# Hybrid decoder layer: one VectorE product moved two slots up, and a state load issued earlier by GpSimd

## The reference, cut to what matters

```python
u = concat([gq, gk, gv])                     # pre-conv rows; the sample group has a cached halo of 3 rows
conv = silu(causal_depthwise_conv(u, conv_w))
q_g, k_g, v_g = l2norm(cq) * GDN_SCALE, l2norm(ck), cv
# per chunk of 64 tokens: solve (I + A) X = rhs with A strictly lower triangular, then update the state
o_gdn, s_gdn_new = gdn_scan(q_g, k_g, v_g, log_a, beta, state_gdn)
o_gdn = rmsnorm(o_gdn, gdn_norm_g) * silu(gz)        # silu(z) for each of a pair's two heads
merged = sigmoid(gate_a) * (o_hg @ w_out_hg) + sigmoid(gate_b) * (o_gdn @ w_out_gdn)
```

## Time and profile before

| what | value |
|---|---|
| median of three runs | 3566.07 us |
| the profiled execution's own time | 3569.11 us |
| its span, first to last instruction | 3567.6 us |
| TensorE matmul busy | 3483.7 us (98%) |
| VectorE / ScalarE / GpSimd busy | 2237.2 (63%) / 1797.9 (50%) / 846.7 (24%) us |
| moved by DMA | 588.08 MB, mean 165 GB/s |
| granted TensorE clock, mean | 0.994 |

### The profile page before, as it was taken

The page is one execution under the profiler, slowest core; times in us unless marked ns, Lnnn a source line. Parts: engine busy times, 40 slices in busy tenths (PEclk is TensorE's granted clock), DMA queues, the critical chain, the costliest instruction groups (busy, mean ns, idle before and its releaser), DMA issues.

```text
span 3567.6 us, 76959 instructions
## 1 busy us (share of the span) xinstructions
PE 3483.7 (98%) x24605; PEld 3173.8 (89%) x24605; DVE 2237.2 (63%) x4307; ACT 1797.9 (50%) x3735; POOL 846.7 (24%) x995
## 2 busy tenths in 40 slices
PE   8999999999999999999999999998998999999998
PEld 2599999998889999998899999996787999999998
DVE  2476666646677777776677777556666555555555
ACT  1245455555545555555555555554565445444454
POOL 2122222201145555450245544311000000000000
PEclk9999999999999999999999999999999999999999
DMA  8655555568844434448644334478874555555554
GB/s 285 207 148 160 144 160 150 155 180 255 257 109 116 116 108 125 122 120 265 183 121 120 111 109 129 120 214 261 243 230 122 166 162 164 165 161 168 160 164 138
DMA packets 884546, 588.08 MB, mean 165 GB/s; under 512 B 23427, under 2 KB 816037, under 8 KB 884165
## 3 DMA queue, kind: packets, MB, share of 16 engines
q1 hardware_dynamic: 857828, 510.50, 49.9%
q0 software_dynamic: 26624, 76.41, 7.6%
HBM read 545.83 MB, written 40.99 MB: 164 GB/s over the span
## 4 chain that ended last, share of the span: by engine, by line
PE 91%; DVE 3%; DMA 3%; issue 2%; ACT 1%; DVEq 0%; ACTq 0%; POOL 0%; SPq 0%; POOLq 0%
PE acc L602 23%; PE acc L604 22%; PE acc L603 22%; PE acc L574 3%; PE bank L792 2%; PE bank L805 2%; PE bank L842 2%; PE bank L826 1%; DMA raw<-in_w_ada 1%; DVE wlo L1521 1%; ACT whi L1027 1%; PE bank L614 1%; DMA raw<-in_w_out_gdn 1%; PE bank L615 1%; PE bank L863 1%
## 5 line engine op out<-in xcount | busy, mean ns | idle before, releaser
L1521 DVE TENSOR_TENSOR wlo<-raw,whi 128x512 fp32r<-128x512 f32 x1799 | 1304.2, 742 | 851.9 <-ACT whi L1027 840.7
L1027 ACT ACTIVATE whi<-raw 128x512 fp32r<-128x512 f32 x1799 | 1095.8, 627 | 869.2 <-PE acc L604 822.4
L602 PE MATMUL acc<-ahi,whi 128*128 128x288 f32 x4112 | 1288.9, 313 | 15.0 <-DVE alo L2035 9.2
L603 PE MATMUL acc<-alo,whi 128*128 128x288 f32 x4112 | 1215.4, 296 | 0.0
L604 PE MATMUL acc<-ahi,wlo 128*128 128x288 f32 x4112 | 1211.6, 295 | 0.0
L602 PEld LDWEIGHTS acc<-ahi,whi 128*128 128x128 f32 x4112 | 775.6, 189 | 37.6 <-issue 26.1
L603 PEld LDWEIGHTS acc<-alo,whi 128*128 128x128 f32 x4112 | 776.7, 189 | 13.3 <-issue 11.5
L604 PEld LDWEIGHTS acc<-ahi,wlo 128*128 128x128 f32 x4112 | 776.0, 189 | 0.0
L602 PE MATMUL acc<-ohi,whi 128*128 128x288 f32 x1792 | 535.5, 299 | 9.5 <-DVE wlo L1521 9.4
L603 PE MATMUL acc<-olo,whi 128*128 128x288 f32 x1792 | 530.1, 296 | 0.0
L604 PE MATMUL acc<-ohi,wlo 128*128 128x288 f32 x1792 | 528.6, 295 | 0.0
(11 more groups left out here) (431 smaller groups left out, 4378.3 us busy)
## 6 DMA issues: line engine op xcount, KB each, us to landing
raw<-in_w_in SPq DMA_DIRECT2D x386, 512.0 KB, 4.1
raw<-in_w_ada SPq DMA_DIRECT2D x192, 512.0 KB, 4.6
raw<-in_w_up SPq DMA_DIRECT2D x128, 512.0 KB, 4.1
raw<-in_w_down SPq DMA_DIRECT2D x128, 512.0 KB, 4.0
raw<-in_w_out_gdn SPq DMA_DIRECT2D x64, 512.0 KB, 5.0
raw<-in_w_o SPq DMA_DIRECT2D x34, 512.0 KB, 4.6
raw<-in_w_out_hg SPq DMA_DIRECT2D x32, 512.0 KB, 5.3
g_S<-in_state_gdn POOLq DMA_DIRECT2D x32, 512.0 KB, 6.6
```

What stands on the lines that cost most here:

```text
L602: mm(bank[:, 0:T], whi[:, s, r, :], hi[:, kt, :], start=(kt == 0), stop=False, skip_group_check=True)
L603: mm(bank[:, 0:T], whi[:, s, r, :], lo[:, kt, :], start=False, stop=False, skip_group_check=True)
L1027: f(whi[:, s], raw[:, r], ACT.Copy).then_inc(sg["hi_made"], 1)
L1521: tt_(wlo[:, s], raw[:, r], whi[:, s].bitcast(F32), SUB).then_inc(sg["lo_made"], 1)
```

## The change

`silu_z(2n+2, 1)` is called in slot 5 of `delta_prev` and not in slot 7, so its product stands ahead of the halo copy of `delta_own`, the two subtractions, the transpose and the split of slot 6. And GpSimd calls `load_delta(0)` straight after `load_cache(0)`, ahead of the last two turns of `merged_out` and the last two stores.

```diff
             def delta_prev(s, n, slot):
-                if s == 7:
+                if s == 5:
                     silu_z(2 * n + 2, 1)
...
             pool.wait_ge(sg["g_zero"], 1)
             load_cache(0)
+            load_delta(0)
             with pool.Fori(KT // 2 - 2, KT // 2) as n:
                 merged_out(n)
             for k in range(2):
                 at = pos(S_WA + KT - 2)
                 pool.wait_ge(sg[f"acc_free{at.bank(k)}"], at.drained(k) + 1)
                 save(merged_d, KT - 2 + k, k)
-            load_delta(0)
             pool.wait_ge(sg["g_halo_turned"], 1)
             load_cache(1)
```

## The result

The changed kernel takes 3592.24 us (median of six runs, 3589.3 to 3594.27) beside 3567.29 us for the kernel before on the same chip (six runs, 3563.81 to 3571.16). The ratio is 1.007 [1.006, 1.0081]: 0.7% slower, about 25 us. The forecast was 3583.5 us with a range up to 3588: the sign is right, and the time lies 4 us above the range. The profiled execution took 3585.92 us, 6.3 us less than the median and less than any of the six, so sizes in its trace are on the low side; before's profiled execution was 1.8 us above its median.

A forecast was written before the change was run, and what follows sets the result against it. TensorE's matmuls, busy 98% of the span, were taken as the bound. 3569.11 + 16.4 (product) + 1.0 (load) = 3586.5 us for the profiled execution, 3.0 above the median, so about 3583.5 us; range 3567 to 3588.

The forecast's parts named there:

- GpSimd goes first: Slot 5 of a GDN body: waiting L2325 runs ahead of the moved product, stopping TensorE 1.11 to 1.46 us; chance 0.66.
- The pair of the earlier trace: First GDN body: behind a split stretched to 5.26 us, GpSimd's L2316 went first; the product ended 0.32 us behind it.
- the stretched split ahead: Slot 4: its split is stretched (1.78 us against 0.69 in slot 8), so the case where GpSimd went first was taken.
- Size in the bodies: TensorE's stops at L792 over the GDN bodies: 6 x 1.20 + 7 x 1.11 + 1.46 = 16.4 us.
- n = 15: Last body, no halo copy, only L1880 ahead of L1881: product behind L2325, TensorE stops 1.46 us.
- The slack of 0.27 us: From VectorE's L1881 to TensorE's L792 in n = 2: anything beyond 0.27 us put ahead of L1881 stops TensorE.
- nothing to gain in slot 7: At the old place the product cost nothing: VectorE sat idle 1.89 us after it until ScalarE's next whi.
- nothing in n = 0 and 8: In these bodies GpSimd is idle or issues DMAs and VectorE waited for TensorE, so no loss there.
- nothing given back later: Later in a body, splits, conv and the inverse's further steps wait for TensorE and move with it, recovering nothing.
- what is left is bandwidth: Load issued at about 908.2 instead of 954.8: only its bandwidth costs, bounds 0 and 3.7 us, 1.0 taken.
- the row of the old place: Window holding the load before: DMA share 1.01, TensorE busy 10.00 of 10 us, pricing the load at nothing.
- The rival in which the load starves the weights: The load's 3.7 us reach TensorE in full and nothing else happens: 3569.8 us; chance alone 0.04.

The follow-up runs named there:

- the kernel with the cache load first: Kernel before with the product in slot 5, load at its old place, GpSimd's load_cache issued ahead of level 3 (L2325): 3573.02 us, ratio 1.0013.
- the product alone: Kernel before with silu_z moved to slot 5 and load_delta(0) left at its old place: 3586.40 us, ratio 1.005.
- the load alone: Kernel before with load_delta(0) moved forward and the product left in slot 7: 3576.03 us, ratio 1.0021; run again 3571.29 us, ratio 1.0011.

## Why the prediction was right, and where it was wrong

**GpSimd goes first: right.** The forecast said L1863 about 1.5 us, L2325 still 1.73, the product's end 0.32 us behind it, L1881's signal 0.12 us. Measured: 1.54, 1.72, 0.32, 0.11. The pair of the earlier trace rows was the right precedent and the earlier trace rows the wrong one. The reason given for the choice, the stretched split ahead, was in part luck: the split of slot 4 is stretched, 1.68 us, but in the kernel with the cache load first GpSimd also went ahead behind splits of 0.70 us. That kernel shows that this wait is the cost in the eleven bodies where its loss went to zero; n = 1 stays unexplained. That the engines exclude each other was read from durations; what they share was not tried.

**Size in the bodies: right.** 16.4 us were forecast. The bodies of the kernel after lose 17.0, less the 1.0 that belongs to the load: 16.0. In the product alone they lose 19.7, less 3.1 for the clock in n = 15: 16.6. The waits of L792 were to be about fourteen and some 15 us; they are 15 and 13.4, one of them the 0.7 us of before. By the times the product costs 17.8 us [12.5, 22.8].

**n = 15: right size, wrong working.** I had the product wait for L2325. In fact the order there has a split between: the product starts at 2273.32, takes 3.09 us, and the split behind it takes 1.77 us until 2278.10, just behind L2325 (2276.06 + 1.49 = 2277.55). The stop is still about 1.5 us, because L1881 waits for the end of L2325 and what stands between in either order. While the product waited, four products of GpSimd that had all started later (from 2273.83 on) ended ahead of it: to have started first doesn't give the turn.

**The slack of 0.27 us, nothing to gain in slot 7, nothing in n = 0 and 8, nothing given back later: right.** The mean loss of 1.1 to 1.2 us in a body is what the sum with this slack gave. The table has 0.0 where the product stands behind L1881, and the stretch between the two groups of bodies, 1602 to 1815, gives back 0.1 us in the kernel after and 0.3 in the product alone.

**The load: the step that failed.** It is the step "what is left is bandwidth": bounds of 0 and 3.7 us, the upper one the price of 1.05 MB at 285 GB/s, and 1.0 taken, by the row of the old place. Measured by the traces the load costs 3.3 + 1.1 = 4.4 and 2.5 + 1.0 = 3.5 us alone, 6.5 and 8.4 with the product, each with 0.3 to 1.1 us of chance in it; by the times 7.5 and 3.9 us alone (0.0021 and 0.0011 of the kernel), and 7.2 as the difference of the whole change and the product (25.0 - 17.8). The forecast of TensorE's loss from 905 to 955 was 1 us; it grew by 3.8 in the windows. With the base of six runs, the 16.4 us of the bodies and the full 3.7 us of the upper bound the time would be 3587.4, inside the range: what carried it out is that in the whole change the load costs more than that bound. The reason given, that only bandwidth is left, was the wrong question. Three things were missed. The weight loads issued just behind the state's land 3 to 5 us later, and TensorE comes to wait for them in S_WA. The place of the load decided, and the row of 955 to 965 in the earlier trace rows that I took as the nearest is of another stage with another use of its weights: the nearest row in kind, not in place. And behind a stop in one piece a stretch at the lower clock can follow, 1.6 us of loss in the trace after, which no bound from the bytes holds.

The rival in which the load starves the weights had 3.7 us and "nothing else happens", with a chance of 0.04. Its mechanism is what happened, on top of the first case: my own note that the two make 3586 us stood beside it. Its size was too small as well.

The Trainium skill (SBUF — State Buffer, A bandwidth-pool intuition that's wrong) states about 358 GB/s of HBM for a core, and by the estimate from it the term would have been nothing. The load alone moved 319 and 323 GB/s in the windows from 915, below that limit, and TensorE still stopped there for 1.1 to 3.0 us: the traces don't agree with the estimate that I made of this load's price.

**The base: 1.2 us.** The median of three runs was 3566.07; of six it is 3567.29, so the profiled execution lay 1.8 us above the median and not 3.0.

The miss of 3592.2 - 3583.5 = 8.7 us falls into 1.2 (base) + 1.4 (product, 17.8 against 16.4) + 6.2 (load, 7.2 against 1.0) = 8.8. That it closes proves nothing, since the 7.2 is taken as the rest; the load alone has 3.9 and 7.5, and the 1.4 of the product lies inside its interval.

**What stays open.** What decides whose turn it is between VectorE and GpSimd, and what the product waited for in n = 1 of the kernel with the cache load first. Whether one half of the load costs as much as both: the times can't tell them apart, and behind one half the weights landed 2.3 us later, behind both 3.4 to 4.9. Whether the stretch at the lower clock follows from the length of a stop was not tried by itself; in n = 15 a stop of 1.5 us came with it once and without it three times, and the 1.9 us of the load alone came without it. And the 1.0 us in n = 3. It stands at L740 in each of the five traces with the load moved and in no other; in the load alone GpSimd has a gap ahead of the store in that body:

```profile
1276.06 0.89 POOL L2353 DMA_DIRECT2D out<-g_S  x1 [0.88 <-issue]
```

and VectorE's conv beside the products behind it takes 4.03 us for three steps where it took 2.41 before. What makes the gap is not known; the kernel before has one like it, 0.84 us, at 1123.

No kernel here beats the one before; the one with the product behind L1881 equals it.

## What to carry to other kernels

When an instruction is moved across a boundary between engines, look for the instruction of the other engine that stands in line at the new place, and price the moved one by pairs of the trace in which the two engines meet in the same way, for either order: it may cost its neighbour's duration, not its own. Price a moved load by what it adds to the landing of the loads beside it, against what the ring covers at that very place, and not by bytes over bandwidth; a neighbouring stage with the same DMA share can have another cover. A stop of the matmul engine in one piece of some 3 us may cost half as much again through its clock, as it did after, where 1.6 us followed 3.3.

## What the runs showed that I had not expected

- A 512 KB weight load took 5.1 to 5.5 us (medians) from issue to landing from 905 to 925 before, some 7 to 9 us just behind one 512 KB load of GpSimd's queue and some 8 to 10 us behind two, though the core moved about as much in sum (5.78 MB after against 5.76 before in these 20 us).
- Half of that load can't be told from the whole by its time: 0.15% against 0.11 and 0.21%.
- Behind a stop of 3.3 us fourteen matmuls started 0.24 us apart instead of 0.13, and the ten microseconds behind a stop of 1.5 us had a granted clock of 0.68 in one execution and 1.00 in three others at the same place.
- GpSimd went ahead of the moved product in all fourteen bodies of the kernel after. Behind an unstretched split VectorE kept its turn in the earlier trace rows and lost it in three bodies of the kernel with the cache load first.
